# Delta rule: keys keep their length, queries' root in the scan, no token stage

## The reference, cut to what matters

```
qkv = silu(centred_conv(qkv, conv_w))          # 5 taps
q, k = l2norm(q), l2norm(k)                    # x * rsqrt(sum(x*x) + EPS), per token and head
beta = sigmoid(beta_logit)
# per chunk of tokens, q scaled by DK ** -0.5:
a_mat = strict_lower((k * beta) @ k.T * decay)
t_mat = inverse(eye + a_mat)
u = t_mat @ (v * beta);   w = t_mat @ (k * beta * exp(gc))
v_new = u - w @ s
o = (q * exp(gc)) @ s + lower(q @ k.T * decay) @ v_new
s = s * exp(g_last) + (k * exp(g_last - gc)).T @ v_new
```

## Time and profile before

| | us |
|---|---|
| median of 3 runs | 2856.4 |
| lowest, highest | 2854.1, 2860.43 |
| profiled execution | 2855.78 |
| its span | 2854.0 |
| busy: PE, DVE, POOL, ACT | 2598.5, 1660.1, 1132.1, 646.7 |
| mean granted TensorE clock | 0.959 |

### The profile page before, as it was taken

How to read it: one execution, slowest core, us unless ns; L and a number is a source line. 1 busy time by engine, 2 the same in 40 slices (tenths; PEclk the granted TensorE clock), 3 DMA queues, 4 the chain that set the end, 5 groups by cost and what they waited for, 6 DMA issues and landing times. The chain is left out here.

```text
span 2854.0 us, 45433 instructions
## 1 busy us (share of the span) xinstructions
PE 2598.5 (91%) x18610; PEld 2172.5 (76%) x18610; DVE 1660.1 (58%) x2509; ACT 646.7 (23%) x1253; POOL 1132.1 (40%) x922
## 2 busy tenths in 40 slices
PE   8989999989889999987699959977798999899998
PEld 6778888777578888776588848864587788688887
DVE  7858668473558758576555655533476615463351
ACT  4122012101322112233443244311254210110000
POOL 3545554453045555432321332211333444444553
PEclk9999999999999999998899979988999999999999
DMA  4224343321033343210011101011200222223232
GB/s 153 103 93 151 111 150 124 117 74 60 1 133 133 123 143 134 86 63 31 24 40 46 59 16 33 32 35 41 52 23 6 104 89 103 87 75 103 89 103 74
DMA packets 51316, 229.68 MB, mean 80 GB/s; under 512 B 5296, under 2 KB 12480, under 8 KB 32576
## 3 DMA queue, kind: packets, MB, share of 16 engines
q1 hardware_dynamic: 51136, 227.10, 23.2%
HBM read 224.91 MB, written 2.17 MB: 80 GB/s over the span
## 5 line engine op out<-in xcount | busy, mean ns | idle before, releaser
L246 POOL TENSOR_TENSOR ring_rounded<-ring,ring_rounded 128x512 fp32r<-128x512 f32 (+2 forms) x715 | 937.5, 1342 | 1152.6 <-DVE ring_rounded L237 1141.9
L286 PE MATMUL psum<-arena_rounded,ring_rounded 128*128 128x512 f32 (+1 forms) x2820 | 1098.8, 390 | 63.4 <-PEq L515 13.7
L287 PE MATMUL psum<-arena_rounded,ring_rounded 128*128 128x512 f32 (+1 forms) x2820 | 1090.9, 387 | 0.0
L288 PE MATMUL psum<-arena_rounded,ring_rounded 128*128 128x512 f32 (+1 forms) x2820 | 1089.6, 386 | 0.0
L286 PEld LDWEIGHTS psum<-arena_rounded,ring_rounded 128*128 128x128 f32 x2820 | 536.5, 190 | 185.9 <-issue 47.6
L288 PEld LDWEIGHTS psum<-arena_rounded,ring_rounded 128*128 128x128 f32 x2820 | 536.2, 190 | 107.7
L287 PEld LDWEIGHTS psum<-arena_rounded,ring_rounded 128*128 128x128 f32 x2820 | 536.8, 190 | 105.0 <-issue 1.5
L237 DVE CAST ring_rounded<-ring 128x2048 fp32r<-128x2048 f32 (+4 forms) x191 | 212.4, 1112 | 686.4 <-PE psum L288 625.0
L713 ACT ACTIVATE arena<-psum,vectors 128x512 f32<-128x512 f32 x88 | 68.6, 782 | 409.0 <-PE psum L288 409.0
L329 DVE TENSOR_TENSOR arena_rounded<-arena,arena_rounded 128x512 fp32r<-128x512 f32 (+2 forms) x113 | 125.3, 1108 | 3.9
L327 DVE CAST arena_rounded<-arena 128x512 fp32r<-128x512 f32 (+2 forms) x113 | 114.1, 1010 | 9.2 <-DVE arena L743 1.0
(11 more groups left out here) (394 smaller groups left out, 3054.3 us busy)
## 6 DMA issues: line engine op xcount, KB each, us to landing
ring<-in_w_up SPq DMA_DIRECT2D x44, 1024.0 KB, 4.8
arena<-in_w_mod SPq DMA_DIRECT2D x48, 512.0 KB, 3.4
ring<-in_w_down SPq DMA_DIRECT2D x32, 704.0 KB, 3.9
ring<-in_w_mup SPq DMA_DIRECT2D x16, 1024.0 KB, 4.8
ring<-in_w_mdown SPq DMA_DIRECT2D x16, 1024.0 KB, 4.8
ring<-in_w_gdn SPq DMA_DIRECT2D x12, 1024.0 KB, 4.9
ring<-in_w_lru_in SPq DMA_DIRECT2D x10, 1024.0 KB, 4.8
ring<-in_w_odd_in SPq DMA_DIRECT2D x10, 1024.0 KB, 4.8
```

The lines of the kernel that those rows point to most:

```text
L246: last = pool.tensor_tensor(self.rounded(low), raw, self.rounded(high).bitcast(F32), ALU.subtract)
L286: pe.matmul(out, r(wh), r(xh), start=start, stop=False)
L287: pe.matmul(out, r(wh), r(xl), start=False, stop=False)
L288: return pe.matmul(out, r(wl), r(xh), start=False, stop=stop)
```

## The change

The weights' order becomes keys, values, queries. The token stage is gone. Turns of keys stand between the first queries unit's products, turns of values between the second's, three in each tile (`queries`, `turn_keys`, `turn_values`), with ScalarE's copies (`token`) in between. Keys are never multiplied by their root. GpSimd squares the six tiles of keys, VectorE sums them behind unit 3's taps (`key_sums`), GpSimd takes pow -0.5 of 24 columns, and `key_roots` makes a Newton step, the key's length, and multiplies beta by the root's square. In the scan, GpSimd multiplies the values by the key's length (`lengthen`). The queries' root moves into the scan: squares on ScalarE, 16 column sums on TensorE, pow on GpSimd, Newton on VectorE, the root spread by TensorE and multiplied into the queries by VectorE before the first `query_gram`. The kept split of the next weights moves into the scan (VectorE at tile 0, level 2; GpSimd at tile 2). Tiles of the scan get other places in SBUF.

```diff
-KTOK_AT, VTOK_AT = 0, 3072
+K_SS, K_ROOT, K_TMP, K_LEN, K_HALF = 64, 88, 112, 136, 160
+Q_MEAN, Q_ROOT, Q_TMP = 24, 40, 64
...
+class TokenTiles:
...
+        self.k_at = tail[0:4] + own[0:2]
+        self.v_at = tail[4:7] + [17408] + own[2:4]
...
-    parts = [1, 1, 0, 0, 2, 2]
+    parts = [1, 1, 2, 2, 0, 0]
...
+        def turn(src, n, bank):
+            for h in range(GH):
+                last = pe.transpose(m.psum[:, bank, h * P:(h + 1) * P], src[:, h, nt(n)], m.ident[:, :])
+            last.then_inc(m.up("turned"), 1)
+
+        def turn_keys(n):
+            if n == 0:
+                pe.wait_ge(m.sem("silu"), m.count("silu", 4))
+            else:
+                pe.wait_ge(m.sem("tokcopied"), m.count("tokcopied", n))
+            turn(outs[1], n, tokbank(n))
+
+        def turn_values(n):
+            if n == 0:
+                pe.wait_ge(m.sem("silu"), m.count("silu", 8))
+                pe.wait_ge(m.sem("tokcopied"), m.count("tokcopied", NA))
+            if n >= 2:
+                pe.wait_ge(m.sem("tokcopied"), m.count("tokcopied", NA + n - 1))
+            turn(outs[2], n, tokbank(NA + n))
+
+        def queries(unit, beside):
+            pe.wait_ge(m.lo_done, unit.g + 1)
+            for t in range(2):
+                for k in range(KD):
+                    last = tile(unit, t, k, 0)
+                    if k in (1, 3, 5):
+                        beside(3 * t + k // 2)
+                last.then_inc(m.up("done"), 1)
...
+        tap(us[4], 0)
+        tap(us[4], 1)
+        token(6)
+        token(7)
+        token(8)
+        tap(us[5], 0)
+        silu(us[4], 0)
+        token(9)
+        silu(us[4], 1)
+        token(10)
+        token(11)
+        tap(us[5], 1)
+        silu(us[5], 0)
+        silu(us[5], 1)
...
+        def key_sums():
+            for n in range(NA):
+                dve.wait_ge(m.sem("squared"), m.count("squared", n + 1))
+                dve.tensor_reduce(kss[:, GH * n:GH * n + GH], ksq[n % 2], AX.X, ALU.add).then_inc(m.up("reduced"), 1)
+            dve.wait_ge(m.sem("reduced"), m.count("reduced", NA))
+            dve.tensor_scalar(kss, kss, EPS, None, ALU.add).then_inc(m.up("kmean"), 1)
+
+        def key_roots():
+            dve.wait_ge(m.sem("kroot"), m.count("kroot", 1))
+            dve.wait_ge(m.sem("kmean"), m.count("kmean", 1))
+            rstd_newton(m, dve, kss, kroot, ktmp, c)
+            dve.wait_ge(c.sem, c.now())
+            dve.tensor_tensor(klen, kss, kroot, ALU.mult).then_inc(c.up(), 1)
+            dve.tensor_tensor(ktmp, kroot, kroot, ALU.mult).then_inc(c.up(), 1)
+            dve.wait_ge(c.sem, c.now())
+            if bd:
+                dve.wait_ge(m.sem("beta"), m.count("beta", 1))
+            squares = ktmp.rearrange("p (n h) -> p n h", h=GH)
+            beta = cols(BETA).rearrange("p (n d h) -> p n d h", d=2, h=8)
+            for d in range(2):
+                b = beta[:, :, d, GH * group:GH * group + GH]
+                dve.tensor_tensor(b, b, squares, ALU.mult).then_inc(m.up("kscaled"), 1)
...
-        for unit in us:
+        dve.memset(khalf, -0.5).then_inc(m.up("khalf"), 1)
+        for unit in us[:5]:
             begin(unit)
-            taps_of(unit)
+            if unit.u == 4:
+                if bd:
+                    turned()
+                key_roots()
+            taps_of(unit, 0)
+            taps_of(unit, 1)
...
+            if unit.u == 3:
+                key_sums()
+        taps_of(us[5], 0)
+        begin(us[5])
+        taps_of(us[5], 1)
...
-        for unit in us:
+        for unit in us[:4]:
+            m.pool_unit(pool, unit)
+        for n in range(NA):
+            pool.wait_ge(m.sem("tokcopied"), m.count("tokcopied", n + 1))
+            if n >= 2:
+                pool.wait_ge(m.sem("reduced"), m.count("reduced", n - 1))
+            pool.tensor_tensor(ksq[n % 2], tok.k(n), tok.k(n), ALU.mult).then_inc(m.up("squared"), 1)
+        pool.wait_ge(m.sem("khalf"), m.count("khalf", 1))
+        pool.wait_ge(m.sem("kmean"), m.count("kmean", 1))
+        pool.tensor_tensor(kroot, kss, khalf, ALU.pow).then_inc(m.up("kroot"), 1)
+        pool.wait_ge(m.sem("kscaled"), m.count("kscaled", 2))
+        for unit in us[4:]:
             m.pool_unit(pool, unit)
...
-def gdn_token_stage(m):
...
         def query_gram(t, d):
             n = tiles[d][t]
             pe.wait_ge(sem("tri", d), count("tri", d, t))
+            pe.wait_ge(m.sem("qscaled"), m.count("qscaled", GH))
...
-            rhs = b["R"] if t else vtok[:, n]
+            else:
+                pe.wait_ge(m.sem("vlong"), m.count("vlong", 2))
+            rhs = b["R"] if t else tok.v(n)
...
+        def query_sums():
+            pe.wait_ge(sem("tri", 0), count("tri", 0, 1))
+            pe.wait_ge(m.sem("qsquare"), m.count("qsquare", GH))
+            for h in range(GH):
+                for i in range(NT):
+                    j = NT * h + i
+                    last = pe.matmul(m.psum[:, MB, j:j + 1], qsq[h][:, i * P:(i + 1) * P], m.ones[:, 0:1],
+                                     start=True, stop=True)
+            last.then_inc(m.up("qsums"), 1)
+
+        def query_spread(h):
+            d = h % 2
+            if h < 2:
+                pe.wait_ge(sem("tri", d), count("tri", d, 2))
+                pe.wait_ge(m.sem("qrstd"), m.count("qrstd", 1))
+            else:
+                pe.wait_ge(m.sem("qscaled"), m.count("qscaled", h - 1))
...
             for k in range(1, LEVELS + 1):
                 left(t, k)
+                if (t, k) == (0, 1):
+                    query_sums()
+                if (t, k) in ((0, 5), (1, 1)):
+                    query_spread(2 * t)
+                    query_spread(2 * t + 1)
...
+        for h in range(GH):
+            act.activation(qsq[h], qt[:, h, :], ACT.Square).then_inc(m.up("qsquare"), 1)
...
+        def lengthen(n):
+            r = klen[:, GH * n:GH * n + GH].rearrange("p (a b) -> p a b", b=1).broadcast_to([P, GH, P])
+            pool.tensor_tensor(tok.v(n), tok.v(n), r, ALU.mult).then_inc(m.up("vlong"), 1)
+
...
+        lengthen(4)
+        lengthen(5)
...
+            if t == 0:
+                pool.wait_ge(m.sem("qmean"), m.count("qmean", 1))
+                pool.tensor_tensor(qroot, qmean, qhalf, ALU.pow).then_inc(m.up("qroot"), 1)
...
+            if t < 2:
+                lengthen(t)
+                lengthen(3 - t)
+            if t == 2:
+                m.pool_kept(pool)
...
+            dve.wait_ge(m.sem("vlong"), m.count("vlong", min(2 * t, NA)))
...
+        def query_roots():
+            dve.wait_ge(m.sem("qroot"), m.count("qroot", 1))
+            rstd_newton(m, dve, qmean, qroot, qtmp, m.vchain)
+            dve.wait_ge(m.vchain.sem, m.vchain.now())
+            dve.tensor_scalar(qroot, qroot, DK ** -0.5, None, ALU.mult).then_inc(m.up("qrstd"), 1)
+
+        def query_scaled(h):
+            dve.wait_ge(m.sem("qspread"), m.count("qspread", h + 1))
+            dve.tensor_tensor(qt[:, h, :], qt[:, h, :], m.psum[:, 4 * (h % 2) + MB, :], ALU.mult).then_inc(
+                m.up("qscaled"), 1)
...
+                if (t, k) == (0, 1):
+                    dve.wait_ge(m.sem("qsums"), m.count("qsums", 1))
+                    dve.tensor_scalar(qmean, m.psum[:, MB, 0:GH * NT], EPS, None, ALU.add).then_inc(
+                        m.up("qmean"), 1)
+                if (t, k) == (0, 2):
+                    m.dve_kept(dve)
+                if (t, k) == (0, 4):
+                    query_roots()
+                if (t, k) in ((0, 5), (1, 1)):
+                    query_scaled(2 * t)
+                    query_scaled(2 * t + 1)
...
     for g in range(2):
         gdn_in_stage(m, S[f"gdn{g}"], S["bd"] if g == 0 else None, v, g, d["gc_rows"])
-        gdn_token_stage(m)
         gdn_scan_stage(m, g, d["gc_rows"])
...
-        f[f"w_gdn{g}"] = units_of(qkv, [8 * part + 4 * g + h for part in (1, 0, 2) for h in range(4)], 8, 2)
+        f[f"w_gdn{g}"] = units_of(qkv, [8 * part + 4 * g + h for part in (1, 2, 0) for h in range(4)], 8, 2)
```

More of the change, by code:

```diff
@@ L1522, with __init__, k, v @@
 GC_ROWS_AT = 17408 + 6 * 96
+class TokenTiles:
+    def __init__(self, m, group):
+        own = [O_AT + GH * T * group + GH * P * i for i in range(4)]
+        tail = [S_AT + GH * P * i for i in range(7)]
+        self.m = m
+        self.k_at = tail[0:4] + own[0:2]
+        self.v_at = tail[4:7] + [17408] + own[2:4]
+    def k(self, n):
+        return self.m.at(self.k_at[n], GH, P)
+    def v(self, n):
+        return self.m.at(self.v_at[n], GH, P)
 def round_xn(m, act, xh):
@@ L1681, in gdn_in_stage @@
     us = unrolled(seg)
-    parts = [1, 1, 0, 0, 2, 2]
+    parts = [1, 1, 2, 2, 0, 0]
+    tok = TokenTiles(m, group)
+    kss, kroot, ktmp, klen, khalf = [m.small[:, a:a + GH * NA] for a in (K_SS, K_ROOT, K_TMP, K_LEN, K_HALF)]
+    ksq = [tok.v(4), tok.v(5)]
+    nt = lambda n: slice(n * P, (n + 1) * P)
     halves = lambda k: (xh[:, k, :], xl[:, k, :])
@@ L1809, in begin, with taps_of @@
             m.dve_unit(dve, unit)
```

(27 more changed lines are left out.)

167 lines of the change are left out of this document (58 added, 109 removed).

## The result

The changed kernel takes 2814.9 us (median of 4 runs, 2812.8 to 2819.0); the kernel before, run beside it, 2858.1 (2854.1 to 2860.4). The ratio is 0.985, with a 95% interval of 0.9835 to 0.9869. The forecast was 2801, range 2791 to 2814: the kernel became faster, as said, but by 41 us of span and not by 55. The profiled execution took 2814.47, its span 2812.6.

What follows compares the result with a forecast made beforehand. It took hand-over chains in the token stages, TensorE then VectorE in the input stages, and small products and masks in the scans as bounds; -55.5 - 6.0 + 1.2 + 5.3 = -55.0 us gave 2801, range 2791 to 2814.

Steps and rivals of the forecast that it cites:

- the price of the column sums: Scan, level 1 on TensorE: 16 sums cost 1.9 to 3.8 us less 1.0 idle; 1.5 taken first scan, 2.8 second.
- The scans: Both scans: new work for the queries' root mostly hidden in waits; they give back 2.0 + 3.3 = 5.3 us.
- the price of the turns: Input stages, TensorE: 48 turns at 0.14 us, 6.7 us between the queries' products, hidden under VectorE's chain.
- The 0.5 a scan for the rest: Scans: spreads, cast, Newton steps and scalings lie in gaps and waits; 0.5 us a scan for what sticks out.
- The second input stage: Second head group: unit 3 ends at 1618.7, VectorE's chain at 1655.1 against 1653.9 before, +1.2 us.
- The two token stages: Between input stages and scans: both go whole, 27.4 + 28.1 = 55.5 us removed.
- The decays' wait: First input stage: the 5.06 us wait for VectorE's column work for the decays goes, as unit 3 ends at 1302.1.
- VectorE ended the input stage: End of input stages: VectorE's chain runs 36.4 us from unit 3's end, 37.3 in the first group, ending there at 1339.4.
- TensorE ends the input stages: Rival, input stages: a cheap pow of 1.96 us leaves turns and products level or last; -5.0 at most, 2796; chance 0.13.
- Cast ahead of pow: Rival, input stage after key_sums: VectorE's cast holds up GpSimd's pow by its whole length, 2 x 1.23, 2803.5; chance 0.25.
- the line between 1.96 and 6.27: Input stage, GpSimd's pow on 24 columns: interpolated between 10 and 32 columns as 4.7 us, 4.9 with hand-over.
- the scan gives back more: Rival, scans: one late hand-over moves the level; 11.2 us a scan if nothing hides, 2818, likelier 2810; chance 0.16.

Runs made afterwards that it cites:

- the fourth experiment: Changed kernel with key_roots behind the first queries unit's taps on VectorE instead of ahead of them, nothing left out; 2806.6 us, ratio 0.9828.
- both edits: Changed kernel with the column sums ahead of the scan's first transform and the first queries unit's taps ahead of key_roots; 2795.0 us, ratio 0.9788.
- the first fill: Kernel with both edits plus 18 unread 128x128 products at the end of unit 5's queries in each input stage; 2797.1 us, ratio 0.9789.
- the last two versions: Kernel with both edits plus 18 unread products ending unit 5's queries, and 18 (2787.2 us) or 12 (2786.3 us) more behind the column sums.
- both places filled: Kernel with both edits plus 18 unread products ending unit 5's queries and 18 behind the column sums; 2787.2 us, ratio 0.9761.

## Why the prediction missed

**The step that failed** is the price of the column sums, under "The scans": "Nearest row: 16 products of 128 x 128 in 2.05 at full clock, 0.12 from start to start". The row has x16, but the code at that line issues one product for each of four heads and two directions: 8 products. A product of fp32 operands stands in the trace as two records (the gram's 8 as x16, 16 column sums as x32, 8-product spreads as x16 in 2.46 and 2.05 us). The row gives 0.12 us a record, so 0.24 a product, and 16 sums are 3.8 at full clock and up to twice that at half; measured, 3.87 and 6.98. I had 1.9 and 3.8. The transposes (L1918) are single records, so the price of the turns had no such error: 0.14 given, and 0.11 measured (four of them push the next product back by 0.45 us).

**The second half of the same step** is the clock. I gave the first scan full clock because it had it by 1388; that is 15 us behind the scan's start. After the change TensorE waits 6.14 us before the first scan, is at 0.50 when it begins, and stays there until about 1369, for 29 us. The sums themselves are part of that: with one sum, or without the queries' root, the clock rose some 20 us behind the scan's start, with the sums twice only after 37. So the first scan paid 7.4 us between levels 1 and 2 where 1.5 was allowed: 5.9 for the sums (10.54 - 4.63, the step with one sum) and 1.5 for the other products at half clock (4.63 - 3.18). From level 2 to 3 it paid 1.2 more. In the second scan two errors met: 2.8 allowed by half the records at half the clock, 2.7 measured with all records at nearly full clock (0.94 while the sums ran) on top of a step that had been 4.61 at half clock before and is 3.17 at full clock with the sums early. The agreement is an accident.

**The 0.5 a scan for the rest** was too little: the step from level 5 to the next tile, where the first spreads stand, went from 6.74 to 8.02 and 7.73. Only the second of these can be put down to the spreads: without the queries' root the step is 6.76 in the second scan but 8.09 in the first, so there another cause, which was not looked for, makes it as long. The spreads take 2.46 and 2.05 in place of the 1.0 given. With the sums moved away, what was left of the queries' root was 2804.0 - 2797.7 = 6.3 us over both scans.

**The second input stage** lost 2.0 us against the forecast. Of these, 1.6 lie in its first unit: from the stage's start to VectorE's next cast 20.5 us (18.9 before), with granted clocks of 0.80 and 0.78 in the first 8 us where all windows before show 1.00. Why the clock is lower there was not tried.

**What was right.** The two token stages went whole. The decays' wait vanished: the last product of unit 3 ended at 1302.0 (forecast 1302.1). VectorE ended the input stage (the fourth experiment shows it), at 1339.6 where 1339.4 was forecast. The lengthening, the kept split and the casts cost nothing in the scans: the kernel without the queries' root has scans as long as before. Nor do the squares (2.17 us, no table load): level 1 comes 14.4 us behind the scan's start with them and 14.5 before. TensorE's own end of the first input stage was 1333.4, with 1332.7 summed, but by errors that offset each other: the gate sums took 0.6 where 1.6 was given and the turns 0.11 each, while the last turn waited 1.90 for ScalarE, which that sum leaves out. The rival "TensorE ends the input stages" fell with the pow, which was not cheap.

**Cast ahead of pow** stood as a rival with 2 x 1.23. The pow is held up by 0.83 in each group, two thirds of it. The Trainium skill, "SBUF — State Buffer", section "Who interferes with whom", says that whichever of a VectorE cast in a two-port mode and a GpSimd instruction is issued first has the shared ports for its whole length; the trace agrees in kind, with 0.83 lost of 0.98 us of overlap. My sum without it came close only because 4.7 by the line between 1.96 and 6.27 was too high for an undisturbed pow of 4.18, and too low by 0.3 for the disturbed one. The mechanism was the rival's, the total the forecast's by luck.

**The range** ended at 2814, the middle of the rival "the scan gives back more". That rival named the mechanism (one late hand-over on an engine served in order moves the level) and its times, 2810 to 2818, hold the result; but it was worked out with the same 3.8 us for the sums and with nothing of the new work hidden, so that its total fits is partly luck.

## What stays open

From level 1 of the second tile to level 1 of the fifth takes 77.0 us where nothing is lost (76.1 without the queries' root; 78.3 and 76.1 before). In the traced execution of the changed kernel it takes 79.6 in the first scan, most of it around the fourth tile, with TensorE idle for 1.38 us that the trace puts down to nothing. The same stretch is 81.2 us in the first scan with the sums early, 81.9 in the second with one sum, 81.4 in the first with both edits and 81.5 in the second with the first fill; the last two versions lose nothing there (at most 0.1). Whether that belongs to the kernels or to the single executions, and whether it makes the wide spread of some of them, was not tried; part of the gain of the last two may be this. The two fastest versions differ by 0.9 us, less than either one's spread, so which fill is better is open.

## What to carry to other kernels

Before a count in a row becomes a price, count the products in the code at that line: an fp32 product stands as two records here, and one that writes a single column costs nearly as much as one that writes 128. Work that is added to a chain of engines served in order belongs in a wait whose length is known (here 7 us ahead of the seeds), not in front of the next link, where a gap of 0.9 us looked free. And price each stretch at the clock that it will have after the change: here the input stage ends on VectorE, and TensorE stood at half clock through all of the next stage's first 29 us, while a full clock handed over (the first fill) was lost again in the wait before the seeds.

## What the runs showed of the hardware

A 128 x 128 by 128 x 1 product takes nearly as long as one of 128 columns. Per record, the single columns took 3.87 / 32 = 0.12 us in the second scan and 6.98 / 32 = 0.22 in the first, the gram 2.05 / 16 = 0.13 and 3.75 / 16 = 0.23. The Trainium skill, "TensorE: Matmul & The Clock Gate", section "LDWEIGHTS (loading the stationary operand)", has the cost of a weight load go by the columns that are loaded, 128 in all of these; that fits the rows.

The clock didn't rise while single-column products filled TensorE. In the kernel with the sums twice, they ran for 13.8 us without a gap, all at the spacing of 0.50, in both scans. With both places filled, TensorE was busy in all of 1338 to 1346, and yet the granted clock fell to 0.64 in the second half of it, right behind the sums:

```profile
1338.00:1342.00 4.00, 4.00 (x35) 4.00 (x36) 1.11 (x4) 2.94 (x9) 2.48 (x2) 0.93 0.39 134
1342.00:1346.00 4.00, 4.00 (x25) 4.00 (x25) 2.91 (x10) 0.08 (x1) 1.71 (x3) 0.64 0.00 2
1346.00:1350.00 4.00, 3.06 (x86) 2.27 (x89) 0.76 (x2) 0.66 (x2) 4.00 (x4) 1.00 0.01 4
```

A VectorE operation of 16 columns can take 0.96 us. Kernel after, VectorE and then GpSimd in the first scan:

```profile
1375.51 0.93 DVE L357 TENSOR_TENSOR small<-small 128x16 f32<-128x16 f32 x1
1376.48 0.96 DVE L359 TENSOR_SCALAR small<-small 128x16 f32<-128x16 f32 x1
1377.47 0.17 DVE L361 TENSOR_TENSOR small<-small 128x16 f32<-128x16 f32 x1
```

```profile
1375.37 1.04 POOL L2395 TENSOR_TENSOR tail<-tail,small 128x512 f32<-128x512 f32 x1
1376.37 1.04 POOL L2395 TENSOR_TENSOR arena<-arena,small 128x512 f32<-128x512 f32 x1
```

Each of the two ends with GpSimd's instruction (1376.44 and 1376.41; 1377.44 and 1377.41), and the third, beside nothing, takes 0.17. It cost nothing here, since these steps lie in VectorE's waits.

GpSimd's pow goes by the column: 1.96 us for 10 columns, 2.91 for 16 and 4.18 for 24 undisturbed, which is 0.16 us a column in both steps ((2.91 - 1.96) / 6, (4.18 - 2.91) / 8). The 32 columns at 6.27 lie 0.8 above that line, which is why interpolating between 10 and 32 gave 4.7 for 24. What lengthened the 32 was not tried.
